# The first modulation set fetched as scale blocks and then shift blocks, channel products in two halves, and the last two expert blocks by columns

## The chip, the cores and the metric

The kernel runs on one NeuronCore of a Trainium2 chip. The metric is the device time of one execution in microseconds (us). Three runs of the kernel before took 1420.25 to 1420.28 us, median 1420.26 us.

## The reference, cut to what matters

Two transformer blocks act on 256 latent and 256 context tokens of 1024 channels, all in float32. The first block has two layers. Layer 0 is an FNet mixer (a DFT over tokens and over channels, then a projection), layer 1 is attention; each is followed by a SwiGLU of 2816. The second block is one mixer (RG-LRU and gated linear attention) and a mixture of 32 experts of which each token uses two, then a last RMS norm.

```python
sh1, sc1, g1, sh2, sc2, g2 = jnp.split(cond_lat @ w_ada[i] + b_ada[i], 6, axis=-1)
h_lat = modulate(rms_norm(x, norm_gain[i, 0]), sh1, sc1)      # y * (1 + sc1) + sh1
o_lat, o_ctx = fnet_mixer(h_lat, h_ctx, fnet_w_out[j], fnet_b_out[j], need_ctx)
x = x + g1 * o_lat
...
hid = jax.nn.silu(xb @ w_gate[e]) * (xb @ w_up[e])            # per expert, on its tokens
y = zeros.at[buf_t].add((hid @ w_down[e]) * buf_w)            # scattered back, weighted
x = x + gt2 * y
return rms_norm_2(x, g_final)
```

Every layer's six modulation vectors (shift, scale and gate, twice) come from a product of a condition vector with a 1024 x 6144 matrix, so the matrix has to be read in full for two columns of data.

## The kernel before

All weights come through one DMA queue (SP) in an order fixed by the list `STREAM`, in blocks of 128 x 2048 floats (1 MB). Each block has a slot; SP waits until the slot's last user has released it and then issues, in order. The other engines (PE, ACT, DVE, POOL) run fixed programs in order too and wait on semaphores, so the order of the code is the order of the work.

**The front.** The first 24 blocks go to eight slots. Their order is: eight blocks `("ada", 0, 0, k)` (k is a depth of 128 rows; the 2048 columns are shift and scale together), `fnet` 0, gate blocks `("ada", 0, 1, 0)` and 1, `fnet` 1, gate blocks 2 and 3, `fnet` 2, `fnet` 3, and eight blocks `("ada", 0, 2, k)`. After `fnet` 2 the tokens `xT` (2 MB) are read by the same queue. PE computes the DFT over tokens (`spectrum(c, streams)`, L977) for eight channel chunks c and two streams (latent, context), from token squares that ACT has made. Between the spectra it takes the `ada` blocks as they land (`ada_rows(n, ks)`, L886: four products of 32 rows a block, eight instructions in the profile, since one float32 matmul is two). When a set is complete, ACT copies the four rows out (`arow_of`, L1826), PE turns them into columns (`ada_cols`, L914 and L916), DVE adds the bias (`mods`, L2400) and, for set 0, makes the gains (L2468). ACT and DVE then scale the spectra by gain into `Z` (L1881, L2532), DVE adds the shift to one column of each chunk (`shift_spectrum`, L2541), and PE does the DFT over channels: `channels(i)` (L987, products of 64 output rows, a cosine and a sine half) and `nyquist` (L992). ACT and DVE split the result into high and low parts (`yh` L1889, `yl` L2555).

POOL folds each `fnet` weight block in four quarters (L2327) as soon as it has landed; ACT and DVE split each quarter in a high part `whi` (L1820) and a low part `wlo` (L2388). PE then runs eight `fnet_chunk(c)` (L1010, L1016), 27 products each; chunks 2b and 2b+1 use `fnet` block b. `MODS` says which `ada_rows` follow which chunk, and `ada_cols(1)` (the gate) comes after chunk 1. ACT and DVE finish each chunk (`join`, `add_fnet`), and the feed-forward follows.

**The experts.** Pairs p = 0 to 15 of experts work side by side, each on 64 slots, as two column groups of the PE array (`side_by_side`, L1627). For a pair: gate and up products, their product turned (L1672), the down product in two halves of 512 columns (`down`, banks 6 and 7), high and low parts of it (ACT `outs` L2282, DVE `outs` L3189), and a scatter back to tokens (`scatter(p, half)`, L1701: eight products into the accumulators of four chunks). Twelve blocks of 1 MB go through per pair. The last four blocks of the stream, `LAST`, are each sent as two DMAs of half a block.

**The tail.** PE: `down(15)` half 0, half 1, `scatter(15, 0)`, `scatter(15, 1)`, then eight sums of squares (`pe_sums`, L865). DVE adds each chunk to x (`added_last`, L3118), ACT squares it (L1831), and after the sums makes the root (L1840, L1842); DVE normalises (`normed(6)`, L2492, eight operations), and SP stores three pieces.

Of the kernel before, what the change touches and what calls it, by code (L numbers as in the profile page):

```python
# [15 lines left out]
P = 128  # L16
# [79 lines left out]
PE_ROWS = {0: range(8), 1: range(4), 2: range(8), 6: range(2), 7: range(1), 8: range(1)}  # L96
# [3 lines left out]
MOD_STREAMS = {n: 2 if n in (0, 1, 2, "g2", 3) else 1 for n in ORDER}  # L100
TWO_DEPTHS = (1, "g2")
# [34 lines left out]
LAST = MOE[-4:]  # L136
LOWER_FIRST = {0: False, 2: False, 6: True, 8: True, 12: True, 14: True, 16: True, 18: True}
# [57 lines left out]
def program(nc, wblk, cols_d, cons_d, small_d, wa2_d, xin_d, xnat_d, dft_d, wny_d, rope_d, out_d):  # L195
    ctx = ExitStack()
    with ctx:
# [262 lines left out]
        s_zero = signal("cleared", [("cact",), ("wny",), ("eps",), ("pick",), ("lx",), ("sT",)])  # L460

        events = []
        for n, (layer, s) in enumerate(SETS):
            if n == 3:
                events.append([("sum", "g2"), ("rows", "g2")])
            mine = [[(n, k)] for k in PE_ROWS.get(n, ())] + [[("sum", n)]] * (layer > 0)
            mine[-1].append(("rows", n))
            events += mine
# [7 lines left out]
        def modulated(layer, s, chunk6):  # L476
            return s_mod.at(3 * layer + chunk6 // 2 if layer else (0, 0, 1, 2, 2, "g2")[chunk6], s)
# [3 lines left out]
        s_sqa = signal("squares_act", [(r, c) for r in range(1, 5) for c in ACT_SQUARES[r]] + [(6, c) for c in range(KC)])  # L481
# [5 lines left out]
        triples = [(r, c, s) for r in (1, 2, 3, 4, 6) for c in range(KC) for s in range(len(NORM_STREAMS[r]))]  # L487
        s_ny = signal("normed", triples)
# [9 lines left out]
        s_d1 = signal("dft_tokens", [(c,) for c in range(KC)])  # L498
        ACT_SCALED, DVE_SCALED = (0, 2, 4, 6, 7), (1, 3, 5)
# [92 lines left out]
        r_sc = signal("r_scattered", [(p, half) for p in range(NP) for half in range(2)])  # L592
# [9 lines left out]
        r_oh = signal("r_out_high", [(p, half) for p in range(NP) for half in range(2)])  # L602
        r_ol = signal("r_out_low", [(p, half) for p in range(NP) for half in range(2)])
# [33 lines left out]
        def turned_rows(n):  # L637
            return bank[{0: 7, 6: 5}.get(n, 6)]
# [139 lines left out]
        def sync(e):  # L778
            def used(tag):
                if tag[0] == "fnet":  # L780
                    e.wait_ge(*s_fold.at(tag[1], 3))
                elif tag[0] == "ada":
                    signal = s_adv if tag[1] == 1 else s_adw if tag[1] == 2 and tag[2:] in WEIGHED else s_adam
                    if tag[1:3] == (0, 3):
                        e.wait_ge(*s_adv.at("g2", tag[3]))
                    else:
                        e.wait_ge(*signal.at(3 * tag[1] + tag[2], tag[3]))
# [81 lines left out]
        def pe(e):  # L869
# [4 lines left out]
            def ada_rows(n, ks):  # L874
                layer, s = SETS[n]
                for k in ks:
                    tag = ("ada", layer, s, k)
                    w = block_of(tag)
                    e.wait_ge(*landed(tag))
                    if k == 0 and n:  # L880
                        e.wait_ge(*s_arow.at(n - 1))
                        if n == 1:
                            e.wait_ge(*s_za.at(7))
                    for g in range(4):
                        depth = 2 * k + g // 2 if n == 1 else k
                        t = e.matmul(bank[7][32 * g:32 * g + 32, :], cact[:, 1 if layer == 2 else 0, depth, :], w[:, g * 512:(g + 1) * 512],  # L886
                                     start=k == 0, stop=k == (3 if n == 1 else 7), skip_group_check=layer == 2)
# [140 lines left out]
            spectrum(3, (1,))  # L1028
            spectrum(4, (0,))
            ada_rows(0, (4,))  # L1030
            spectrum(4, (1,))
            ada_rows(0, (5,))
            spectrum(5, (0,))
            ada_rows(0, (6,))
# [12 lines left out]
            channels(3)  # L1047
            nyquist(1)
            ada_rows(1, range(1, 2))
            MODS = {0: (1, range(2, 4)), 3: (2, range(1)), 4: (2, range(1, 3)), 5: (2, range(3, 5)), 6: (2, range(5, 6))}  # L1050
            for c in range(KC):
# [3 lines left out]
                if c == 1:  # L1055
# [558 lines left out]
        def pe_routed(e):  # L1614
# [67 lines left out]

            def down(p):
                lhs = lambda k, i: hidT[:, p % 2, k, 64 * i:64 * i + 64]
                e.wait_ge(*r_hidT.at(p))
                for half in range(2):
# [5 lines left out]
                    if p == NP - 1 and half:  # L1692
                        scatter(p, 0)


# [9 lines left out]
            for p in range(NP + 2):  # L1705
# [7 lines left out]
                if p > NP:  # L1713
                    scatter(NP - 1, 1)
# [13 lines left out]
            pe_sums(e, 6)  # L1728
# [1687 lines left out]
```

## Time and profile before

| | |
|---|---|
| median of three runs | 1420.26 us |
| the profiled execution's own time | 1419.94 us |
| its span, first to last instruction | 1418.0 us |
| PE busy | 1379.8 us (97%) |
| DVE, ACT, POOL busy | 789.1, 524.2, 75.8 us |
| granted TensorE clock, mean | 0.998 |
| HBM | 388.01 MB read, 274 GB/s over the span |

The span runs from the first to the last instruction; the remaining 1.94 us of the profiled execution lie around it. Busy time of PE is modelled from pipelined starts, so it says where PE had nothing to do rather than how well it was used. In the front and in the expert stage the DMA engines are busy throughout; between them they are not.

### The profile page before, as it was taken

Reading aid. Unit: us, or ns where it says so; the run is one execution under the profiler, and the core shown is the slowest. Engines: PE = TensorE matmul, PEld = TensorE weight load, DVE = VectorE, ACT = ScalarE, POOL = GpSimd, SP = SyncE. Lnnn points to the kernel's source line nnn. Section 1 sums busy time; section 2 is a strip of 40 time slices with the busy share of each in tenths; the row PEclk is TensorE's granted clock in tenths of the full one; section 3 lists DMA queues with packets and bytes.
Section 4 is the critical chain, followed back from the end, with each engine's and each line's share of the span. In section 5 each row is a group of like instructions: output and inputs, shape, how many; then the busy total and the mean of one; then the engine's idle time right before and its main releaser. Section 6 shows DMA issues by size and latency. Waiting matters only on the chain.

```text
span 1418.0 us, 20093 instructions
## 1 busy us (share of the span) xinstructions
PE 1379.8 (97%) x8038; PEld 994.2 (70%) x8038; DVE 789.1 (56%) x1402; ACT 524.2 (37%) x1099; POOL 75.8 (5%) x74
## 2 busy tenths in 40 slices
PE   7999999999999999999999999999999999999987
PEld 4767887888887998888888998996444444443433
DVE  1978796665666886667788778684212112112113
ACT  2643222223444555445556666852111111111102
POOL 0600000000002141000000000010000000000000
PEclk9999999999999999999999999999999999999999
DMA  9958666764443332013687454478999999999995
GB/s 391 425 220 314 237 249 256 267 241 174 167 175 119 149 129 81 31 60 117 264 340 318 150 208 178 179 305 324 425 432 428 430 430 428 429 432 429 430 427 224
DMA packets 48130, 390.42 MB, mean 275 GB/s; under 512 B 5256, under 2 KB 6552, under 8 KB 9376
## 3 DMA queue, kind: packets, MB, share of 16 engines
q1 hardware_dynamic: 47408, 387.70, 68.1%
q8 instruction: 66, 1.08, 0.3%
q10 hardware_dynamic: 624, 1.37, 0.2%
q14 instruction: 32, 0.26, 0.1%
HBM read 388.01 MB, written 1.05 MB: 274 GB/s over the span
## 4 chain that ended last, share of the span: by engine, by line
PE 85%; DMA 8%; DVE 3%; ACT 2%; issue 1%; SPq 0%; DVEq 0%; ACTq 0%
PE twin L966 41%; PE twin L1627 19%; DMA ring<-in_wblk 6%; PE twin L1064 5%; PE twin L1065 3%; PE twin L1701 2%; DMA front_ring<-in_wblk 2%; PE twin L1610 2%; PE twin L1010 2%; PE twin L1480 2%; PE twin L1305 1%; PE twin L1241 1%; PE twin L1265 1%; DVE wlo L2388 1%; PE twin L886 1%
## 5 line engine op out<-in xcount | busy, mean ns | idle before, releaser
L2388 DVE TENSOR_TENSOR wlo<-ring,whi 128x512 fp32r<-128x512 f32 (+1 forms) x392 | 254.4, 697 | 64.7 <-ACT whi L1820 61.7
L1820 ACT ACTIVATE whi<-ring 128x512 fp32r<-128x512 f32 (+1 forms) x392 | 216.8, 611 | 106.7 <-PE twin L966 86.4
L966 PE MATMUL twin<-H,whi 128*128 128x512 f32 x700 | 216.3, 390 | 0.1
L966 PE MATMUL twin<-hsp,whi 128*128 128x512 f32 (+1 forms) x704 | 172.5, 337 | 1.8 <-DVE hsp L2587 0.9
L1627 PE MATMUL twin<-ring,xg 128*64 128x512 f32 x696 | 158.3, 597 | 8.4 <-DMA ring<-in_wblk 8.0
L966 PEld LDWEIGHTS twin<-H,whi 128*128 128x128 f32 x700 | 130.8, 188 | 30.1 <-issue 2.5
L966 PE MATMUL twin<-H,wlo 128*128 128x512 f32 x350 | 136.2, 389 | 0.0
L966 PEld LDWEIGHTS twin<-hsp,whi 128*128 128x128 f32 x704 | 120.7, 190 | 17.0 <-DVE wlo L2388 1.7
L1064 PE MATMUL twin<-H,whi 128*128 128x512 f32 x350 | 124.2, 400 | 0.5 <-DVE H L2485 0.2
L966 PE MATMUL twin<-hsp,wlo 128*128 128x512 f32 (+1 forms) x352 | 118.3, 336 | 0.0
L1627 PEld LDWEIGHTS twin<-ring,xg 128*64 128x64 f32 x696 | 48.0, 137 | 97.0 <-issue 88.2
L1627 PE MATMUL twin<-ring,xT 128*64 128x512 f32 x456 | 102.0, 595 | 2.5 <-DMA ring<-in_wblk 2.0
L3174 DVE TENSOR_TENSOR rst<-rst,twin 128x512 f32<-128x512 f32 x16 | 11.0, 688 | 166.4 <-issue 161.2
L1065 PE MATMUL twin<-H,wlo 128*128 128x256 f32 x350 | 98.3, 281 | 0.0
L966 PE MATMUL twin<-whi,Hh 128*128 128x256 f32 x304 | 88.3, 291 | 0.0
L966 PE MATMUL twin<-wlo,Hh 128*128 128x256 f32 x304 | 85.9, 283 | 0.0
L966 PE MATMUL twin<-whi,Hl 128*128 128x256 f32 x304 | 85.9, 283 | 0.0
L3189 DVE SCALAR_TENSOR_TENSOR outs<-twin,tiny,outs 128x512 fp32r<-128x512 f32 x32 | 24.0, 751 | 104.6 <-ACT outs L2282 52.8
L1064 PEld LDWEIGHTS twin<-H,whi 128*128 128x128 f32 x350 | 65.8, 188 | 17.6 <-DVE H L2485 0.6
L2587 DVE TENSOR_TENSOR hsp<-hid,hsp 128x512 fp32r<-128x512 f32 (+1 forms) x88 | 49.1, 563 | 50.5 <-ACT hsp L1928 50.5
L1928 ACT ACTIVATE hsp<-hid 128x512 fp32r<-128x512 f32 (+1 forms) x88 | 45.5, 524 | 84.6 <-PE twin L966 84.6
L1627 PEld LDWEIGHTS twin<-ring,xT 128*64 128x64 f32 x456 | 32.1, 137 | 62.4 <-issue 62.3
(428 smaller groups left out, 2375.6 us busy)
## 6 DMA issues: line engine op xcount, KB each, us to landing
ring<-in_wblk SPq DMA_DIRECT2D x213, 1024.0 KB, 6.1
ring<-in_wblk SPq DMA_DIRECT2D x56, 2048.0 KB, 30.6
front_ring<-in_wblk SPq DMA_DIRECT2D x12, 1024.0 KB, 19.1
small<-in_wblk SPq DMA_DIRECT2D x10, 1024.0 KB, 26.4
tmp<-in_wblk SPq DMA_DIRECT2D x9, 1024.0 KB, 23.8
ring<-in_wblk SPq DMA_DIRECT2D x12, 512.0 KB, 18.8
xnat<-in_xnat SPq DMA_DIRECT2D x4, 512.0 KB, 6.7
xT<-in_xin SPq DMA_DIRECT2D x1, 2048.0 KB, 23.4
```

What stands on the lines that cost most here:

```text
L966: t = e.matmul(out, a, b, start=start and n == 0, stop=stop and n == 2)
L1010: e.matmul(out[:, r], ws[x][:, k, m * P:(m + 1) * P], y[:, i, r], start=k == 0 and n == 0, stop=k == KC - 1 and n == 2, skip_group_check=True)
L1064: e.matmul(b[:, :].rearrange("p (x n) -> p x n", x=2), w[0], FHB[1][:, :, k, :], start=start, stop=stop, skip_group_check=True)
L1065: return e.matmul(b[:, 0:L], w[1], FH[1][0][:, k, :], start=False, stop=stop, skip_group_check=True)
L1480: t = e.matmul(wout_bank(b, m)[:, m * L:(m + 1) * L], ws[i][:, k, m * P:(m + 1) * P], XM[j][:, k, :], start=k == 0 and (m == 0 or b == 3) ...
L1610: t = e.matmul(gather_bank(q, j)[:, i * 256:(i + 1) * 256], h2[n % 2][:, n // 2, c * P:(c + 1) * P], Gs[:, n // 2, :], start=n == 0, stop= ...
L1627: t = e.matmul(like(out[64 * i:64 * i + 64, :], rows), lhs(kcs + kk, i), rows, start=start and kk == 0, stop=stop and kk == 3)
L1701: t = e.matmul(acc(c), osp[:, part_, c * P:(c + 1) * P], Sw[:, p % 2, :], start=p == 0 and part_ == 0 and c % 2 == 0, stop=p == NP - 1 and ...
L1820: e.activation(hi, w, ACT.Copy).then_inc(*s_hi.up(m, h))
L1928: e.activation(hsp[:, k % nsp, 0, 0:n], hid[:, k, 0:n], ACT.Copy).then_inc(*s_hph.up(layer, half, k))
L2388: e.tensor_tensor(lo, w, hi.bitcast(F32), ALU.subtract).then_inc(*s_lov.up(m, h))
L2587: e.tensor_tensor(hsp[:, k % nsp, 1, 0:n], hid[:, k, 0:n], hsp[:, k % nsp, 0, 0:n].bitcast(F32), ALU.subtract).then_inc(*s_hpl.up(layer, h ...
```

## The change

Set 0 is split in two sets that are fetched one behind the other in the same eight places of the stream: four blocks with the scale (each two depths of 1024 columns), then four with the shift. Their rows, columns and `mods` become two steps; the shift has bank 4. Gains and scaled spectra need the scale alone. `channels(i)` is split in the sine half (which no shift touches) and the cosine half. The order of spectra begins with chunk 4. Five products of cleared data go ahead of the first spectrum, and POOL clears their operand first. `MODS` moves some set 1 and set 2 rows one chunk later, and `ada_cols(1)` to behind chunk 2.

The last two blocks hold columns 512 to 767 and 768 to 1023 of both experts' down weights over the whole depth, where they held half the depth of 512 columns. `scatter(15, 0)` is put between the two column products, and the second half's scatter is split in two, with two of the sums of squares between. ACT takes squares 0 to 3 ahead of the last high part, and makes x times final gain for chunks 0 to 3 after it; DVE normalises these four in one operation.

```diff
-ADA0 = {0: (0, 2), 1: (2, 1), 2: (3, 2), "g2": (5, 1)}
-ORDER = [0, 1, 2, "g2", 3, 4, 5, 6, 7, 8]
+ADA0 = {0: (1, 1), "shift": (0, 1), 1: (2, 1), 2: (3, 2), "g2": (5, 1)}
+ORDER = [0, "shift", 1, 2, "g2", 3, 4, 5, 6, 7, 8]
...
+                    if k == 0 and n == "shift":
+                        e.wait_ge(*s_za.at(4))
...
-            def channels(i):
-                e.wait_ge(*s_dc.at(2 * i + 1))
-                for table, r, n0, n1 in ((cd, EVEN, 127, 256), (sd, ODD, 0, 127)):
-                    for j in range(2):
-                        t = e.matmul(streams(spectrum_bank[i][64 * j:64 * j + 64, r]), table, Z[:, 2 * i + j, :, n0:n1], start=True, stop=True)
-                t.then_inc(*s_d2.up(i))
+            def channels(i, r):
+                if r == ODD:
+                    for c in (2 * i, 2 * i + 1):
+                        e.wait_ge(*(s_za if c in ACT_SCALED else s_zv).at(c))
+                else:
+                    e.wait_ge(*s_dc.at(2 * i + 1))
+                table, n0, n1 = (sd, 0, 127) if r == ODD else (cd, 127, 256)
...
-            for c in range(4):
+            e.wait_ge(*s_zero.at("warm"))
+            for _ in range(5):
+                e.matmul(bank[6][:, :], rst[:, 0, 0:P], rst[:, 0, :], start=True, stop=True)
+            for c in (4, 0, 1, 2, 3):
                 spectrum(c, (0,))
+            spectrum(4, (1,))
+            e.wait_ge(*s_cond.at("c2"))
+            ada_rows(0, (0,))
             spectrum(0, (1,))
-            e.wait_ge(*s_cond.at("c2"))
-            ada_rows(0, range(2))
             spectrum(1, (1,))
+            ada_rows(0, (1,))
+            spectrum(2, (1,))
             ada_rows(0, (2,))
-            spectrum(2, (1,))
+            spectrum(3, (1,))
+            spectrum(5, (0,))
             ada_rows(0, (3,))
...
             spectrum(5, (1,))
-            ada_rows(0, (7,))
-            spectrum(6, (0,))
             e.wait_ge(s_cons, 16)
             ada_cols(0)
-            spectrum(6, (1,))
-            spectrum(7)
-            channels(0)
-            channels(1)
+            spectrum(6)
+            spectrum(7, (0,))
+            ada_rows("shift", (0,))
+            spectrum(7, (1,))
+            ada_rows("shift", (1, 2))
+            channels(0, ODD)
+            ada_rows("shift", (3,))
+            channels(1, ODD)
+            ada_cols("shift")
+            channels(2, ODD)
+            channels(3, ODD)
+            channels(0, EVEN)
+            channels(1, EVEN)
             nyquist(0)
-            channels(2)
+            channels(2, EVEN)
             ada_rows(1, range(1))
-            channels(3)
+            channels(3, EVEN)
             nyquist(1)
             ada_rows(1, range(1, 2))
-            MODS = {0: (1, range(2, 4)), 3: (2, range(1)), 4: (2, range(1, 3)), 5: (2, range(3, 5)), 6: (2, range(5, 6))}
+            MODS = {0: (1, range(2, 3)), 1: (1, range(3, 4)), 3: (2, range(1)), 4: (2, range(1, 2)), 5: (2, range(2, 4)), 6: (2, range(4, 6))}
             for c in range(KC):
                 fnet_chunk(c)
                 if c in MODS:
                     ada_rows(*MODS[c])
-                if c == 1:
+                if c == 2:
                     ada_cols(1)
...
+            def last_columns(a):
+                tag = LAST[2 + a]
+                rows = block_of(tag)[:, :].rearrange("p (k i n) -> p k i n", k=4, i=2)
+                out = bank[5 if a else 7][:, 0:L]
+                e.wait_ge(s_upper[2 + a], 16)
+                for k in range(4):
+                    if k == 2:
+                        e.wait_ge(*landed(tag))
+                    for i in range(2):
+                        t = e.matmul(out[64 * i:64 * i + 64, :], hidT[:, (NP - 1) % 2, k, 64 * i:64 * i + 64], rows[:, k, i, :], start=k == 0, stop=k == 3)
+                t.then_inc(*s_rel.up(*tag))
...
-                    if p == NP - 1 and half:
-                        scatter(p, 0)
+                if p == NP - 1:
+                    e.wait_ge(*r_ol.at(p - 1, 1))
+                    last_columns(0)
+                    scatter(p, 0)
+                    last_columns(1)
...
                 if p > NP:
-                    scatter(NP - 1, 1)
+                    scatter_last(0)
+                    pe_sums(e, 6, range(2))
+                    scatter_last(1)
...
-            pe_sums(e, 6)
+            pe_sums(e, 6, range(2, KC))
...
-                if c == 0:
+                if c == 1:
                     arow_of(1)
...
+            def last_gained():
+                for c in range(4):
+                    t = e.activation(xg[:, c, :], xT[:, c, 0:L], ACT.Copy, scale=NORM_A[6, 0][:, c:c + 1])
...
         def pool(e):
+            e.memset(rst[:, 0, :], 0.0).then_inc(*s_zero.up("warm"))
...
+            def last_normed():
+                e.wait_ge(*s_root.at(6))
+                e.wait_ge(*s_sqa.at("gained"))
+                e.tensor_tensor(hM[:, 0:4, :], xg[:, 0:4, :], rst[:, 0, 0:L].unsqueeze(1).broadcast_to([P, 4, L]), ALU.mult).then_inc(*s_ny.up(6, 3, 0))
+                for c in range(4, KC):
+                    e.scalar_tensor_tensor(hM[:, c, :], xT[:, c, 0:L], NORM_A[6, 0][:, c:c + 1], rst[:, 0, 0:L], ALU.mult, ALU.mult).then_inc(*s_ny.up(6, c, 0))
```

## Rows read from the trace of the kernel before

**Rows 1.** The page: the chain that ended last, by engine.

```profile
PE 85%; DMA 8%; DVE 3%; ACT 2%; issue 1%; SPq 0%; DVEq 0%; ACTq 0%
```

**Rows 2.** Timeline of PE, 0 to 75 us: start, length, instructions [idle before, releaser].

```profile
9.54 7.21 PE L977 MATMUL twin<-fs,xnat 128*128 128x256 f32 x20 [9.54 <-DVE fs L2509]
16.68 1.92 PE L886 MATMUL twin<-ring,small 128*32 128x512 f32 x16
18.53 1.13 PE L977 MATMUL twin<-fs,xnat 128*128 128x256 f32 x4
19.59 1.06 PE L886 MATMUL twin<-ring,small 128*32 128x512 f32 x8
...
31.63 1.06 PE L886 MATMUL twin<-front_ring,small 128*32 128x512 f32 x8 [0.82 <-DMA front_ring<-in_wblk]
...
33.60 0.60 PE L916 MATMUL twin<-cons,small 128*128 128x128 f32 x4
34.03 2.76 PE L977 MATMUL twin<-fs,xnat 128*128 128x256 f32 x12
36.72 2.17 PE L987 MATMUL twin<-Z,dft 128*64 128x258 f32 x16
...
43.85 0.39 PE L1010 MATMUL twin<-yh,whi 128*128 128x258 f32 x1
...
47.75 1.92 PE L886 MATMUL twin<-front_ring,small 128*32 128x512 f32 x16
49.60 0.39 PE L1010 MATMUL twin<-yh,whi 128*128 128x258 f32 x1
...
52.94 0.96 PE L914 MATMUL twin<-cons,small 128*128 128x8 f32 x8
...
60.39 1.06 PE L886 MATMUL twin<-ring,small 128*32 128x512 f32 x8
```

**Rows 3.** Timeline of POOL, 0 to 70 us.

```profile
0.73 0.52 POOL L2311 MEMSET small<- 128x512 f32 x1 [0.29 <-POOLq L3296]
...
33.93 4.97 POOL L2327 TENSOR_TENSOR fold<-ring 128x512 f32<-128x512 f32 x4 [31.53 <-DMA ring<-in_wblk]
41.24 6.36 POOL L2327 TENSOR_TENSOR fold<-ring 128x512 f32<-128x512 f32 x4 [2.33 <-DMA ring<-in_wblk]
...
56.11 8.52 POOL L2327 TENSOR_TENSOR fold<-front_ring 128x512 f32<-128x512 f32 x4 [1.33 <-DMA front_ring<-in_wblk]
```

**Rows 4.** Timeline of ACT, 0 to 80 us.

```profile
5.57 1.06 ACT L1863 ACTIVATE Z<-xnat 128x1024 f32<-128x1024 f32 x1 [0.62 <-DMA xnat<-in_xnat]
...
32.77 0.60 ACT L1826 ACTIVATE small<-twin 128x512 f32<-128x512 f32 x1 [18.38 <-PE twin L886]
```

**Rows 5.** Timeline of DVE, 0 to 80 us.

```profile
14.42 1.23 DVE L2511 TENSOR_TENSOR wnl<-tmp,wnh 128x1024 fp32r<-128x1024 f32 x1 [1.76 <-ACT wnh L1875]
34.24 0.26 DVE L2400 TENSOR_TENSOR mod<-twin,cols 128x16 f32<-128x16 f32 x2 [18.59 <-PE twin L916]
...
41.42 1.64 DVE L2388 TENSOR_TENSOR wlo<-fold,whi 128x512 fp32r<-128x512 f32 x1
```

**Rows 6.** Timeline of PE in the expert stage, 1270 to 1388 us.

```profile
1313.65 3.65 PE L1627 MATMUL twin<-ring,xg 128*64 128x512 f32 x16 [2.71 <-DMA ring<-in_wblk]
```

**Rows 7.** Timeline of PE, 1385 us to the end.

```profile
1394.28 2.38 PE L1701 MATMUL twin<-Sw,outs 128*128 128x256 f32 x16
1396.59 7.09 PE L1627 MATMUL twin<-ring,xT 128*64 128x512 f32 x32
1403.60 2.38 PE L1701 MATMUL twin<-Sw,outs 128*128 128x256 f32 x16
1406.09 3.72 PE L865 MATMUL twin<-xT,cons 128*128 128x256 f32 x16
```

**Rows 8.** Stretches of 1 us at the end: length, engines' busy, granted clock, DMA share, GB/s.

```profile
1400.00:1401.00 1.00, 1.00 (x8) 0.36 (x6) 0.00 (x0) 0.66 (x1) 0.00 (x0) 1.00 0.12 49
```

**Rows 9.** Timeline of DVE, 1385 us to the end.

```profile
1410.87 3.25 DVE L2492 SCALAR_TENSOR_TENSOR hTm<-xT,cols,rst 128x256 f32<-128x256 f32 x8 [2.55 <-ACT rst L1842]
```

More of the change, by code:

```diff
@@ L136 @@
 LAST = MOE[-4:]
+OUT_PARTS = [(p, half) for p in range(NP) for half in range(2)][:-1] + [(NP - 1, 1, a) for a in range(2)]
 LOWER_FIRST = {0: False, 2: False, 6: True, 8: True, 12: True, 14: True, 16: True, 18: True}
@@ L465, in program @@
                 events.append([("sum", "g2"), ("rows", "g2")])
+            if n == 1:
+                events += [[("shift", k)] for k in range(3)] + [[("shift", 3), ("rows", "shift")]]
             mine = [[(n, k)] for k in PE_ROWS.get(n, ())] + [[("sum", n)]] * (layer > 0)
@@ L476, in modulated @@
         def modulated(layer, s, chunk6):
-            return s_mod.at(3 * layer + chunk6 // 2 if layer else (0, 0, 1, 2, 2, "g2")[chunk6], s)
-        s_sqa = signal("squares_act", [(r, c) for r in range(1, 5) for c in ACT_SQUARES[r]] + [(6, c) for c in range(KC)])
+            return s_mod.at(3 * layer + chunk6 // 2 if layer else ("shift", 0, 1, 2, 2, "g2")[chunk6], s)
+        s_sqa = signal("squares_act", [(r, c) for r in range(1, 5) for c in ACT_SQUARES[r]] + [(6, c) for c in range(4)] + [("gained",)] + [(6, c) for c in range(4, KC)])
         s_sqv = signal("squares_dve", [(r, c) for r in range(1, 5) for c in range(KC - 1) if c not in ACT_SQUARES[r]] + [(5, KC - 1)])
@@ L497, in program @@
         s_a0 = signal("fnet_scales", [(0,)])
-        s_d1 = signal("dft_tokens", [(c,) for c in range(KC)])
-        ACT_SCALED, DVE_SCALED = (0, 2, 4, 6, 7), (1, 3, 5)
+        s_d1 = signal("dft_tokens", [(c,) for c in (4, 0, 1, 2, 3, 5, 6, 7)])
+        ACT_SCALED, DVE_SCALED = (4, 0, 2, 6, 7), (1, 3, 5)
         s_za = signal("spectrum_scaled_act", [(c,) for c in ACT_SCALED])
@@ L591, in program @@
         r_spp = signal("r_spread", [(p,) for p in range(NP)])
-        r_sc = signal("r_scattered", [(p, half) for p in range(NP) for half in range(2)])
+        r_sc = signal("r_scattered", OUT_PARTS)
         r_sel = signal("r_selected", [(0, 0), (0, 1)] + [(q,) for q in range(1, 8)])
@@ L601, in program @@
         r_gs = signal("r_slot_weights", [(p,) for p in range(NP)])
-        r_oh = signal("r_out_high", [(p, half) for p in range(NP) for half in range(2)])
-        r_ol = signal("r_out_low", [(p, half) for p in range(NP) for half in range(2)])
+        r_oh = signal("r_out_high", OUT_PARTS)
+        r_ol = signal("r_out_low", OUT_PARTS)
         d_dg = signal("d_diagonals", [("dg",)])
@@ L637, in turned_rows, with rows_bank @@
         def turned_rows(n):
-            return bank[{0: 7, 6: 5}.get(n, 6)]
+            return bank[{0: 7, "shift": 4, 6: 5}.get(n, 6)]
+        def rows_bank(n):
+            return bank[4 if n == "shift" else 7]
         def unit_turned(u):
@@ L785, in used @@
                         e.wait_ge(*s_adv.at("g2", tag[3]))
+                    elif tag[1:3] == (0, 0) and tag[3] >= 4:
+                        e.wait_ge(*s_adam.at("shift", tag[3] - 4))
                     else:
@@ L1685, in down @@
                 e.wait_ge(*r_hidT.at(p))
-                for half in range(2):
+                for half in range(1 if p == NP - 1 else 2):
                     if p % 2 == 0 and p < 14:
@@ L1691, in down, with scatter_last @@
                     side_by_side(bank[6 + half], p, "ed", half, 0, lhs, True, True)
-                    if p == NP - 1 and half:
-                        scatter(p, 0)
+                if p == NP - 1:
[3 more added lines that the diff above has]
+                    last_columns(1)
+            def scatter_last(a):
+                for part_ in range(2):
+                    e.wait_ge(*(r_ol if part_ else r_oh).at(NP - 1, 1, a))
+                    for c in range(4 + 2 * a, 6 + 2 * a):
+                        t = e.matmul(acc(c), osp[:, part_, c * P:(c + 1) * P], Sw[:, (NP - 1) % 2, :], start=False, stop=part_ == 1,
+                                     skip_group_check=True)
+                t.then_inc(*r_sc.up(NP - 1, 1, a))
             def scatter(p, half):
@@ L1825, in arow_of @@
                     e.wait_ge(*s_adat.at(BEFORE[i]))
[L1826 removed]
+                e.activation(arow[:, :], rows_bank(i)[:, :], ACT.Copy).then_inc(*s_arow.up(i))
             def square(r, c, ready):
@@ L1886, in act @@
                 scale_spectrum(c)
+            arow_of("shift")
             for i in range(4):
@@ L2278, in act_routed @@
                     for half in range(2):
+                        if (p, half) == (NP, 1):
+                            e.wait_ge(*r_sc.at(p - 2, half))
+                            for a in range(2):
+                                if a:
+                                    before_last()
+                                e.wait_ge(*s_rel.at(*LAST[2 + a]))
+                                e.activation(osp[:, 0, 512 + a * L:512 + (a + 1) * L], bank[5 if a else 7][:, 0:L], ACT.Copy,
+                                             scale=gslot[:, (NP - 1) % 2:(NP - 1) % 2 + 1]).then_inc(*r_oh.up(NP - 1, 1, a))
+                            break
                         e.wait_ge(*s_rel.at("ed", 2 * p - 1, half))
@@ L2543, in dve @@
             e.wait_ge(*s_a0.at(0))
-            scale_spectrum(1)
-            shift_spectrum(0)
-            shift_spectrum(1)
-            scale_spectrum(3)
-            shift_spectrum(2)
-            shift_spectrum(3)
-            scale_spectrum(5)
-            for c in range(4, KC):
+            for c in DVE_SCALED:
+                scale_spectrum(c)
+            mods("shift")
+            e.wait_ge(*s_mod.at("shift", 1))
+            for c in range(KC):
                 shift_spectrum(c)
@@ L3183, in dve_routed @@
                     e.wait_ge(*r_gs.at(p - 1))
-                    for half in range(2):
+                    for half in range(1 if p == NP else 2):
                         r = slice(half * 512, (half + 1) * 512)
@@ L3194, in dve_routed, with low_last @@
                     slot_weights(p + 1)
-            for half in range(2):
-                e.wait_ge(*r_sc.at(NP - 1, half))
-                for c in range(4 * half, 4 * half + 4):
-                    added_last(c)
+            def low_last(a):
+                r = slice(512 + a * L, 512 + (a + 1) * L)
+                e.wait_ge(*r_oh.at(NP - 1, 1, a))
+                e.scalar_tensor_tensor(osp[:, 1, r], bank[5 if a else 7][:, 0:L], gslot[:, (NP - 1) % 2:(NP - 1) % 2 + 1], osp[:, 0, r].bitcast(F32),
+                                       ALU.mult, ALU.subtract).then_inc(*r_ol.up(NP - 1, 1, a))
+            low_last(0)
+            e.wait_ge(*r_sc.at(NP - 1, 0))
+            for c in range(4):
+                added_last(c)
+            low_last(1)
+            for a in range(2):
+                e.wait_ge(*r_sc.at(NP - 1, 1, a))
+                added_last(4 + 2 * a)
+                added_last(5 + 2 * a)
         def dve_dense(e):
```

81 lines of the change are left out of this document (46 added, 35 removed).

## The prediction

> **What bounds the kernel now.** I read the page's chain first: 85% of the path that ends last is PE and 8% DMA [rows 1]. So an edit counts only if it shortens PE's list of work where PE never waits, or brings forward what PE does wait for. The change touches the first 60 us and the last 18. What lies between is tied together: SP issues a block when its slot is released, so an earlier PE gives earlier transfers. The expert stage too, where PE waits for blocks (2.71 us at 1313.65 [rows 6]), moves along as a whole, since its transfers start on released slots. I take a gain in the front to arrive at the end in full.
>
> In the front, PE's timeline [rows 2] shows a list that is nearly dense from 9.54 us, with three losses. The first 20 spectrum products take 7.14 us to the next start, 0.357 each, against 0.224 (2.69 / 12) at 34.03: 2.66 us lost, which looks like 1.2 GHz for most of that stretch and 2.4 GHz after. At 31.63 PE waits 0.82 us for the eighth block. Chunk 0 takes 3.90 us (43.85 to 47.75), chunk 1 3.34: 0.56 us of waits for low parts.
>
> The transfers have a clock of their own. POOL starts each fold when its block lands: 41.24 and 56.11, with six blocks' worth between (two gate blocks, `fnet` 2, 2 MB of `xT`, `fnet` 3) [rows 3], or 2.48 us a block. The change leaves that order as it is. So the first block of set 2, next in the stream, lands at about 56.11 + 2.48 = 58.6 us whatever PE does. PE takes it at 60.39 now.
>
> In the tail PE is dense again [rows 7]: half 1 of the last down product starts at 1396.59 + 7.01 / 2 = 1400.10, the scatters at 1403.60, the sums at 1406.09, ending about 1409.81. That is 9.71 us, of which the scatters have 2.49 where the same 16 took 2.31 at 1394.28, so 0.18 is waiting. DMA has sunk to a share of 0.12 by 1400 to 1401 [rows 8]: the last blocks are there before PE needs them.
>
> **The front, step by step.** I count PE's list up to the start of chunk 3. Before: columns of the gate at 52.94, 0.85 us (0.96 less the overlap with the next), chunk 2 3.34, so 57.13.
> - The five products on cleared data. They go ahead of 9.54, where PE is idle. If they raise the clock, 2.66 us go. Ten instructions of 512 columns at the slow rate would take 0.357 x 2 x 10 = 7.1 us or a little more, from 1.3 us on (one more memset like the 0.52 us one [rows 3]), so they are over by about 8.5 to 9.5. They cost nothing, up to 0.4 us if they run over. The gap to the first spectrum is 0 to 1 us. PE came out of the 2.71 us wait at full rate (16 in 3.65 us [rows 6]), so the gap alone should not lose the clock. POOL's other clears come 0.52 us later; ACT has 0.62 us of waiting for tokens there [rows 4], so nothing, at most 0.5.
> - Scale first. Its four blocks are in 4 x 2.48 us before the eighth, about 21.7. Gains and scaled spectra are made under other spectra. The 0.82 us go, since PE has other work when the eighth block lands.
> - Added: set 0's columns are eight instructions for four transposes (0.85 for 0.43), +0.42, and the shift's columns +0.85. ACT's copy of the shift rows (0.60 [rows 4]) is covered by one sine half, 0.54 (a quarter of 2.17): +0.15. `mods` and two shift steps (0.26 for two `mods` [rows 5]) lie under two more sine halves.
> - More changes of kind: four spectrum instructions standing alone take 1.06 for 0.90, a lone block's rows 1.0 for 0.925. Some five more such seams: +0.5 (bounds 0 and 1).
> - Waits of chunk 0: the shift's chain ends earlier against it, -0.56, at least 0.
>
> Sum: 57.13 - 2.66 - 0.82 - 0.56 + 0.42 + 0.85 + 0.15 + 0.5 = 55.0. Chunk 3 ends at 58.35. There PE wants the first block of set 2, which lands at 58.6. So the front gives 60.39 - 58.6 = **1.8 us**, not the 2.1 that PE's list saves; the transfer becomes the bound. The later blocks (61.1, 63.5, 66.0, 68.5, 71.0) are wanted from 62.9, 67.3 and 72.5 on, so they don't wait. The gate's `mods` now comes behind chunk 2, at about the same time as before on the clock, so DVE's additions lose their lead; the chunks that need them (low parts for 4 and 6) start 1.8 earlier but still after.
>
> **The tail.** PE: the two column products are 16 instructions each, 64 rows by 256 columns. No such row stands here; from below half the pace of the 512-column ones, 7.01 / 64 x 16 = 1.75, from above the channel products, 64 rows by 258 columns, 2.17 [rows 2]. I take 1.95, nearer the middle because those channel products also waited for DVE. PE then needs 3.9 + 2.31 + 3.72 = 9.93 for 9.71: **+0.22** (from -0.2 to +0.66). Moving `scatter(15, 0)` and two sums ahead only reorders a list with 0.18 us of air in it. ACT stays within: its 256-column pieces at 0.4 (under the 0.60 of 512) begin squares at 3.5 after 1400.10, and reach the last square at 8.7, when the last sum starts at 9.46. The four gain products there cost nothing, but 0.7 is all the room.
>
> DVE: eight normalisations take 3.25, 0.41 each [rows 9]. Four of them become one operation of 1024 columns on SBUF data. The like of it took 1.23 [rows 5]; bounds 0.6 (twice that rate) and 1.63 (no gain). With 1.23 the end comes **0.40** sooner. The stores follow. Tail: -0.18 (from -1.2 to +0.66).
>
> **Sum.** 1419.94 (the profiled execution's own time) - 1.80 - 0.18 = 1417.96. The median of the runs is 0.32 above that execution, so 1418.3.
>
> **Where a page would have it otherwise.** The first rows show slow instructions at the start and the expert rows none behind a wait. The Trainium skill (TensorE: Matmul & The Clock Gate, Part 1: The HAM clock gate) says that the throttled clock is the default, released by activity and resumed after idling. By that the products help, if the pause behind them is short; the trace agrees for the long-running array. Low parts show DVE held while POOL folds: 1.64 at 41.42, as POOL began at 41.24 [rows 3, 5]. The Trainium skill (SBUF - State Buffer, SBUF: two separate sides) calls the port pair of the two an exclusive lock for a whole instruction; the third rival is what that would do here.
>
> **The rivals.**
> - *PE's list bounds and is shorter than I sum.* The seams cost nothing (54.5 rather than 55.0) and the first block of set 2 lands a little ahead of the pace. Front 2.6, tail 0.5 with the column products at their lower bound: 3.1, so 1417.2. For it: the landing is inferred, not seen. Against: 2.48 holds over six blocks.
> - *The clock does not rise, or falls again before 9.54.* This is the one on the other side. The list is 2.66 longer, chunk 3 starts at 57.7 and ends at 61.0 where 60.39 stood: +0.6, tail -0.18, so 1420.7. It decides as soon as less than about 0.6 us of the 2.66 is won. For it: two sets of columns are added, and nothing in the trace shows how cleared data acts.
> - *Low parts are late.* Block 0's folding runs 33.93 to 38.90 and block 1's from 41.24 [rows 3], under DVE's high-low work, which now begins some 3 us earlier. If each of the four quarters is held 0.5 to 1 us (1.24 a fold quarter), chunk 0 or 2 waits about 1.4, of which 0.25 is free: 1419.4.
> - *Column products don't run side by side.* Each 256-column instruction at 0.224: 3.6 each, +3.3 on the tail, so 1421.6. Against: the channel products, in the same two groups, do.
>
> **How the numbers follow.** Forecast 0.60 (own range 1417.7 to 1418.9), the shorter list 0.17, low parts 0.10, the clock 0.09, columns 0.04. The likeliest gives 1418.3. The range 1417.0 to 1420.0 leaves out the clock, the columns and the far end of the shorter list. A measurement of this kernel tells 0.2%, 2.84 us, from no change: faster means below 1417.42. That is the shorter list and a corner of the forecast, 0.22; slower, above 1423.1, needs two mishaps, 0.02; same 0.76.
>
> **What would show it.** First 20 spectrum products at 0.224 each from 9.54. PE idle on DMA for some 0.3 us ahead of the first set 2 rows, at 58.6, and none at 31.6. Chunk 0 near 42. Columns 1.95 each; the sums' end 9.9 after the last pair's half 0; one DVE operation of 1.2 us. I am wrong if PE takes that block later than 59.2 or before 58.0, or if the tail from half 0's end to the last normalisation changes by over 0.7.

## The result, and the profile after

The changed kernel takes 1420.84 us (median of 17 runs, 1418.80 to 1424.89), the kernel before in runs on the same chip 1419.22 (17 runs). The ratio is 1.0015, with a 95% interval of 1.0009 to 1.0022: 2.1 us slower (1.3 to 3.1), where 2.0 faster was forecast. The two medians alone differ by 1.6. The profiled execution took 1423.76 us, with a span of 1421.3.

The first thing on the page is the chain of waits by engine, which answers to [rows 1]:

```profile
PE 87%; DMA 6%; DVE 4%; ACT 2%; issue 1%; SPq 0%; DVEq 0%; ACTq 0%
```

DMA has given up two points, and PE and DVE have taken them. So the question is what PE does more of, and where DVE came onto the path. PE's timeline from the start (start, length, instructions, and in brackets the idle time before them with its releaser) answers to [rows 2]:

```profile
1.31 5.97 PE L1036 MATMUL twin<-rst 128*128 128x512 f32 x10 [1.31 <-POOL rst L2382]
9.27 5.45 PE L987 MATMUL twin<-fs,xnat 128*128 128x256 f32 x24 [1.99 <-DVE fs L2581]
14.65 1.07 PE L896 MATMUL twin<-ring,small 128*32 128x512 f32 x8
...
36.59 0.66 PE L1001 MATMUL twin<-Z,dft 128*64 128x258 f32 x4 [0.17 <-DVE Z L2613]
37.82 0.66 PE L1001 MATMUL twin<-Z,dft 128*64 128x258 f32 x4 [0.57 <-DVE Z L2613]
...
42.65 0.39 PE L1025 MATMUL twin<-yh,whi 128*128 128x258 f32 x1
...
54.98 0.96 PE L924 MATMUL twin<-cons,small 128*128 128x8 f32 x8
55.79 0.37 PE L1025 MATMUL twin<-yh,whi 128*128 128x258 f32 x1
...
59.19 1.06 PE L896 MATMUL twin<-ring,small 128*32 128x512 f32 x8
62.64 0.58 PE L1025 MATMUL twin<-yh,whi 128*128 128x258 f32 x1 [2.39 <-DVE wlo L2460]
63.02 0.42 PE L1025 MATMUL twin<-yl,whi 128*128 128x258 f32 x1
```

Down to 59.19 the front does nearly what was forecast: the first 24 spectrum products are over in 5.38 us, chunk 0 begins at 42.65 (43.85 before), and the first rows of set 2 at 59.19 (60.39 before). Then comes a wait that the kernel before does not have: 2.39 us for a low part of `fnet` block 2. And the first products behind it start 0.215 us apart instead of 0.12. The stretches of 1 us around it (length; busy time and instructions of PE, PEld, DVE, ACT, POOL; granted clock; DMA share; GB/s) show why:

```profile
62.00:63.00 1.00, 0.36 (x1) 0.36 (x2) 1.00 (x2) 0.63 (x1) 0.00 (x0) 0.61 1.10 467
63.00:64.00 1.00, 1.00 (x6) 1.00 (x6) 1.00 (x3) 0.00 (x0) 0.00 (x0) 0.50 1.01 426
64.00:65.00 1.00, 1.00 (x7) 1.00 (x6) 1.00 (x3) 0.00 (x0) 0.00 (x0) 0.50 0.97 410
65.00:66.00 1.00, 1.00 (x8) 1.00 (x8) 0.96 (x4) 0.00 (x0) 0.00 (x0) 0.68 1.05 442
```

The granted clock is 0.50, which is 1.2 GHz, for some 3.4 us; it falls at 62.2, while PE still waits. Thirteen products of chunk 4 run at that pace, which costs 13 x (0.215 - 0.12) = 1.2 us. Wait and clock together are 3.6 us, against the 1.2 that the front had gained at 59.19.

What DVE does meanwhile stands in its timeline, here of the kernel before:

```profile
54.47 0.23 DVE L2400 TENSOR_TENSOR mod<-twin,cols 128x8 f32<-128x8 f32 x2
54.74 1.67 DVE L2527 SCALAR_TENSOR_TENSOR xT<-tmp,mod,xT 128x256 f32<-128x256 f32 x4
56.33 2.49 DVE L2388 TENSOR_TENSOR wlo<-fold,whi 128x512 fp32r<-128x512 f32 x4
```

and of the kernel after, with POOL's last fold among it:

```profile
55.97 0.24 DVE L2472 TENSOR_TENSOR mod<-twin,cols 128x8 f32<-128x8 f32 x2 [3.79 <-PE twin L924]
56.09 5.62 POOL L2399 TENSOR_TENSOR fold<-front_ring 128x512 f32<-128x512 f32 x4 [1.70 <-DMA front_ring<-in_wblk]
56.24 5.74 DVE L2599 SCALAR_TENSOR_TENSOR xT<-tmp,mod,xT 128x256 f32<-128x256 f32 x4
61.91 2.48 DVE L2460 TENSOR_TENSOR wlo<-fold,whi 128x512 fp32r<-128x512 f32 x4
```

The same four additions take 1.67 us before POOL's fold and 5.74 us under it, 1.43 each, as long as one quarter of the fold (5.62 / 4 = 1.41). In the kernel before, the fold began at 56.11 [rows 3], while DVE was still in the last addition, and DVE went on to the low parts at 56.33 without a break. They kept their 0.62 each, and it was POOL that waited: the first quarter of its fold took 3.88 us, and the whole fold 8.52. After the change POOL is first by 0.15 us, and DVE waits. The first quarter alone, before and after:

```profile
56.11 3.88 POOL L2327 TENSOR_TENSOR fold<-front_ring 128x512 f32<-128x512 f32 x1 [1.33 <-DMA front_ring<-in_wblk]
```

```profile
56.09 1.31 POOL L2399 TENSOR_TENSOR fold<-front_ring 128x512 f32<-128x512 f32 x1 [1.70 <-DMA front_ring<-in_wblk]
```

The low parts for chunk 4 stand behind the additions in DVE's program, so PE waits too.

The tail answers to [rows 7] and [rows 9]; first PE, then DVE:

```profile
1403.13 1.90 PE L1714 MATMUL twin<-ring,xT 128*64 128x256 f32 x16
1404.96 1.21 PE L1745 MATMUL twin<-Sw,outs 128*128 128x256 f32 x8
1406.09 1.95 PE L1714 MATMUL twin<-ring,xT 128*64 128x256 f32 x16
1407.97 0.74 PE L1736 MATMUL twin<-Sw,outs 128*128 128x256 f32 x4
...
1409.89 2.75 PE L873 MATMUL twin<-xT,cons 128*128 128x256 f32 x12
...
1413.63 1.22 DVE L3192 TENSOR_TENSOR hTm<-xg,rst 128x1024 f32<-128x1024 f32 x1 [2.67 <-ACT rst L1895]
1414.78 1.66 DVE L3194 SCALAR_TENSOR_TENSOR hTm<-xT,cols,rst 128x256 f32<-128x256 f32 x4
```

From 1403.13, where the columns begin, to DVE's end at 1416.44 are 13.31 us. Before, from half 1 at 1400.10 to 1414.12, they were 14.02. That is 0.71 less. But from DVE's end to the end of the span it is now 4.86 us, where it was 3.88.

### The profile page after: what moved, and what is told of

It is laid out like the page before. It is cut to its first block, busy times and chain, and to the rows that moved or that the text cites. A ratio compares the mean times of both kernels' runs of the same rounds, so it can differ in the third digit from the quotient of the medians.

```text
span 1421.3 us, 20182 instructions
## 1 busy us (share of the span) xinstructions
PE 1388.2 (98%) x8076; PEld 999.3 (70%) x8076; DVE 792.0 (56%) x1402; ACT 527.5 (37%) x1105; POOL 72.9 (5%) x75
## 3 DMA queue, kind: packets, MB, share of 16 engines
q8 instruction: 66, 1.08, 0.3%
## 4 chain that ended last, share of the span: by engine, by line
PE 87%; DMA 6%; DVE 4%; ACT 2%; issue 1%; SPq 0%; DVEq 0%; ACTq 0%
PE twin L976 41%; PE twin L1649 19%; DMA ring<-in_wblk 6%; PE twin L1086 5%; PE twin L1087 3%; PE twin L1745 2%; PE twin L1632 2%; PE twin L1025 2%; PE twin L1502 2%; PE twin L896 1%; PE twin L1327 1%; PE twin L1263 1%; PE twin L987 1%; PE twin L1287 1%; DVE wlo L2460 1%
## 5 line engine op out<-in xcount | busy, mean ns | idle before, releaser
L2460 DVE TENSOR_TENSOR wlo<-ring,whi 128x512 fp32r<-128x512 f32 (+1 forms) x392 | 254.4, 697 | 65.2 <-ACT whi L1873 62.2
L1649 PE MATMUL twin<-ring,xT 128*64 128x512 f32 x440 | 98.4, 595 | 2.0 <-DMA ring<-in_wblk 2.0
L976 PEld LDWEIGHTS twin<-H,wlo 128*128 128x128 f32 x350 | 65.7, 188 | 13.8
```

The source lines that it names most:

```text
L976: t = e.matmul(out, a, b, start=start and n == 0, stop=stop and n == 2)
L1649: t = e.matmul(like(out[64 * i:64 * i + 64, :], rows), lhs(kcs + kk, i), rows, start=start and kk == 0, stop=stop and kk == 3)
L2460: e.tensor_tensor(lo, w, hi.bitcast(F32), ALU.subtract).then_inc(*s_lov.up(m, h))
```

## The experiments

Two marks place each run's differences: the start of ACT's last operation on chunk 7's product (the end of the front), and the length from the start of half 1 or the columns to the end of the span (the tail). All ratios are to the kernel before on the same chip. The second run of the changed kernel, gate back, fold waits and tail only were measured on one chip, the four others on a second; the kernel before took 1419.29 us (median of 33 runs) on either. The first row of the changed kernel is the result above, against its own 1419.22. The measured differences are the ratio's, times 1419.3.

| kernel | chunk 7 mark | against before | tail | ratio [95%] | difference, us |
|---|---|---|---|---|---|
| before | 79.83 | | 17.90 | 1 | |
| after | 82.42 | +2.59 | 18.17 | 1.0015 [1.0009, 1.0022] | +2.1 |
| after, again | 82.51 | +2.68 | 18.17 | 1.0010 [1.0000, 1.0021] | +1.4 |
| gate back | 78.27 | -1.56 | 18.36 | 0.9988 [0.9979, 0.9997] | -1.7 |
| fold waits | 78.52 | -1.31 | 18.05 | 0.9989 [0.9980, 0.9998] | -1.6 |
| low parts first | 78.58 | -1.25 | 17.46 | 0.9993 [0.9984, 1.0002] | -1.0 |
| gate back, old tail | 78.29 | -1.54 | 17.8 | 0.9991 [0.9982, 1.0000] | -1.3 |
| gate back, no warm | 79.73 | -0.10 | 17.98 | 1.0004 [0.9995, 1.0013] | +0.6 |
| no warm | 81.31 | +1.48 | 18.44 | 1.0011 [1.0002, 1.0020] | +1.6 |
| tail only | 79.87 | +0.04 | 17.96 | 0.9992 [0.9983, 1.0001] | -1.1 |

**The changed kernel once more.** No edit. Could the wait be an accident of one execution?

> The changed kernel once more, on the chip of the next three, to see which of its stretches come back. Theory (lock): DVE's four additions of chunks 0 and 1 again run against POOL's fold of the last fnet block and take 5 to 6 us (1.67 before), and PE waits 2 to 2.5 us for the low parts of fnet block 2 ahead of chunk 4. Rival (chance): that wait is not there again, and what was slow were the low-clock spells at 929 and 1318 us. By the theory 1.001 to 1.002 of the kernel before, by chance anything from 0.998.

It was not. PE's row in the profile of this run:

```profile
62.53 0.39 PE L1025 MATMUL twin<-yh,whi 128*128 128x258 f32 x1 [2.37 <-DVE wlo L2460]
```

The additions took 5.72 us and the clock fell again behind the wait. This profile's span was 1419.1. The stretch from the mark to the tail took 2.3 us less than in the first profile, which had two more spells of low clock in it (929 to 936 and 1318 to 1322 us). Such spells come and go from run to run; the front's loss is in both profiles.

**Gate back.** The gate's columns again behind chunk 1, with its last block of rows and ACT's copy of the rows one chunk earlier too; the rest of the change kept.

```diff
-            MODS = {0: (1, range(2, 3)), 1: (1, range(3, 4)), 3: ...  # (cut)
+            MODS = {0: (1, range(2, 4)), 3: ...  # (cut)
...
-                if c == 2:
+                if c == 1:
                     ada_cols(1)
...
-                if c == 1:
+                if c == 0:
                     arow_of(1)
```

> The changed kernel with both late gate blocks behind chunk 0 and the gate's columns behind chunk 1, as before. The additions then start some 3.5 us earlier, about 52.5, and are done before POOL starts its last fold at 56.1. Lock theory and the rival that the columns are simply too late both expect the additions in 1.7 us, no wait ahead of chunk 4, chunk 7 over some 3.5 to 4 us earlier than in the changed kernel, and 0.9975 to 0.999 of the kernel before. If the spells of low clock in the middle were the cause, it stays at 1.001.

Measured 1418.37 us. DVE again gets the additions done ahead of the fold, and PE never waits between 55 and 66 us (PE and DVE in order of time):

```profile
51.40 0.96 PE L924 MATMUL twin<-cons,small 128*128 128x8 f32 x8
...
53.59 2.19 DVE L2599 SCALAR_TENSOR_TENSOR xT<-tmp,mod,xT 128x256 f32<-128x256 f32 x4 [0.43 <-DVE mod L2472]
55.70 2.48 DVE L2460 TENSOR_TENSOR wlo<-fold,whi 128x512 fp32r<-128x512 f32 x4
...
58.83 1.06 PE L896 MATMUL twin<-ring,small 128*32 128x512 f32 x8
```

The low parts start at 55.70, ahead of POOL's fold at 56.04, and it is again the fold's first quarter that waits (3.33 us). So the gate's place turns 2.1 us of loss into 1.7 of gain. It does not yet say whether the columns' lateness is enough, or whether the overlap with POOL is needed.

**Fold waits.** The columns stay late. POOL's last fold starts only when the second chunk has been added, so that the overlap alone is gone.

```diff
                 if b >= 2:
                     e.wait_ge(*s_lov.at(b - 2, 3))
+                if b == 3:
+                    e.wait_ge(*s_fnx.at(1, 1))
```

> The changed kernel, with POOL's fold of the last fnet block held until DVE's four additions are done; the gate's columns stay behind chunk 2. Lock theory: the additions start at 56.2 as in the changed kernel but take 1.7 us, DVE's split ends about 60.3, the first low part is there at 58.5, PE waits nothing ahead of chunk 4; POOL folds from 58 to 63.6, early enough for chunk 6. Chunk 7 ends 3.5 us earlier than in the changed kernel; 0.9975 to 0.999 of the kernel before. Rival (columns too late by themselves): the wait ahead of chunk 4 stays at 2 us or more and the time at 1.001.

DVE and POOL of this kernel:

```profile
55.86 0.24 DVE L2474 TENSOR_TENSOR mod<-twin,cols 128x8 f32<-128x8 f32 x2 [3.79 <-PE twin L924]
56.13 1.68 DVE L2601 SCALAR_TENSOR_TENSOR xT<-tmp,mod,xT 128x256 f32<-128x256 f32 x4
57.72 2.49 DVE L2462 TENSOR_TENSOR wlo<-fold,whi 128x512 fp32r<-128x512 f32 x4
...
57.98 8.06 POOL L2401 TENSOR_TENSOR fold<-front_ring 128x512 f32<-128x512 f32 x4 [3.71 <-DVE xT L2601]
```

This is the run that decides, by one added wait. The additions start as late as in the changed kernel (56.13 for 56.24), but take 1.68 us instead of 5.74. The low parts start at 57.72, PE goes from set 2's rows at 59.08 straight into chunk 4 at 60.07, and its clock stays up. The kernel is faster than before by 1.6 us. On the same chip the changed kernel's median was 1421.35, this one's is 1418.18. Against gate back (1418.37) nothing is lost by being late; what the changed kernel loses comes with the overlap. The fold itself, from 57.98 on, took 8.06 us, and PE did not wait for anything made from it.

**Low parts first.** The other way round: the overlap stays, but DVE makes `fnet` block 2's low parts ahead of the additions.

```diff
             join(1)
+            split(12)
             mods(1)
...
             add_fnet(1)
-            split(12)
```

> The changed kernel with DVE's low parts of fnet block 2 ahead of the gate's mods and the additions of chunks 0 and 1. Lock theory: the low parts are there by 55.5, the additions still start at 56.2 and still take 5.7 us against POOL's fold, but PE doesn't wait for them ahead of chunk 4, nor for the next low parts ahead of chunk 6 (about 69 against a start at 69.7, so a wait of up to 0.5 us can show). Chunk 7 ends at 78.5 to 79; 0.9985 to 0.9995 of the kernel before. Rival (additions late hold up the rest of DVE's list): a wait of over 1 us moves to chunk 6 and the time stays at 1.001.

DVE of this kernel:

```profile
52.89 3.63 DVE L2460 TENSOR_TENSOR wlo<-fold,whi 128x512 fp32r<-128x512 f32 x4 [0.76 <-ACT whi L1873]
...
56.70 5.62 DVE L2599 SCALAR_TENSOR_TENSOR xT<-tmp,mod,xT 128x256 f32<-128x256 f32 x4
```

The additions are held just as long, 5.62 us, and PE does not wait (59.13, then chunk 4 at 60.13). Median 1417.40 us, the lowest of all, though the interval still touches no change. So a slow DVE operation is no cost by itself. It became one because four low parts that PE wants at 60.2 stood behind it.

**No warm.** Without the five products on cleared data and their wait, everything else as changed. What are they worth?

> The changed kernel without the five products on cleared data ahead of the first spectrum (POOL's clearing stays). The first 24 spectrum products then take some 8 us, not 5.4, and PE's list reaches chunk 4 about 2.6 us later, near 62.8. Lock theory: DVE's low parts for that chunk come at 62.6 or a little later anyway, so the wait of 2.4 us shrinks to under 1, the low clock behind it goes too, chunk 7 is over at 81 to 82.5 (82.42 in the changed kernel), and the whole takes the same as the changed kernel or up to 1 us less. Rival (PE's list sets the front): 2.6 us slower than the changed kernel, 1.003 of the kernel before.

PE and DVE of this kernel in order of time:

```profile
9.59 7.50 PE L987 MATMUL twin<-fs,xnat 128*128 128x256 f32 x24 [9.59 <-DVE fs L2578]
...
57.76 4.43 DVE L2596 SCALAR_TENSOR_TENSOR xT<-tmp,mod,xT 128x256 f32<-128x256 f32 x4
...
60.70 1.06 PE L896 MATMUL twin<-ring,small 128*32 128x512 f32 x8
62.11 2.48 DVE L2457 TENSOR_TENSOR wlo<-fold,whi 128x512 fp32r<-128x512 f32 x4
...
62.85 0.39 PE L1025 MATMUL twin<-yh,whi 128*128 128x258 f32 x1 [1.08 <-DVE wlo L2457]
```

The 24 products take 7.43 us instead of 5.38, and PE comes to set 2's rows 1.5 us later. But the low parts come when POOL's fold lets DVE go, at 62.11 against 61.91. The 1.5 us that the warm products gave had only made the wait longer, 2.39 instead of 1.08, and with 1.08 the clock did not fall. So the front ends 1.1 us earlier without them. In the medians (1420.78, and 1420.84 and 1421.35 with them) the two kernels are not told apart.

**Gate back, no warm.** Both edits. Here the same five products have nothing behind them that eats their gain.

> The kernel with the gate's columns back behind chunk 1, without the five products. There the low parts are early, so PE's list counts: it reaches the first rows of set 2 about 2.1 us later than with them (60.9 for 58.8, where the block's landing held it), and chunk 7 ends near 80.4 against 78.27. Time 2 us above that kernel: ratio 1.000 to 1.001 of the kernel before. Rival (the products buy nothing anywhere): 0.9988 as with them.

The mark is at 79.73 for 78.27: 1.46 us, and in the medians 1419.63 for 1418.37 (on two chips; by the ratios it is 2.3, and the two intervals just overlap). Worth some 1.3 us in one version and nothing, or less, in the other.

**Tail only.** The new tail on the kernel before.

> The tail of the change alone on the front of the kernel before. From the start of the last down product's second half to DVE's last operation 13.3 us, as in the changed kernel, against 14.0 before (PE's list 9.5 for 9.7, normalising 2.8 for 3.25). Theory: the whole is 0.7 us faster, ratio 0.9995, as the stores take 3.9 us as before. Rival: the stores take 4.9 us, as in the changed kernel's profile, since the third is issued late, and the ratio is 1.000 or above.

From the columns to DVE's end it is 13.31 us, to the hundredth what the changed kernel has. The median is 1418.85 us, -1.1 us with an interval of -2.4 to +0.1; the profile's tail as a whole is no shorter than before (17.96 for 17.90).

**Gate back, old tail.** The tail tested from the other side: the gate-back kernel with the tail of before.

> The kernel with the gate's columns back behind chunk 1, and the tail of the kernel before. From the start of the last down product's second half to DVE's last operation 14.0 us, against 13.3 with the new tail. First theory: the new tail is worth its 0.7 us, so this is 0.7 us slower than the kernel with the gate back (1418.4). Second theory: the stores end at a time of their own, 18.0 to 18.4 us behind that start with either tail, and the two kernels are equal within 0.3 us.

1418.11 us against 1418.37 with the new tail: no difference that can be told. In the profiles, what DVE saves is used up behind it. The span ends 4.1 to 5.1 us behind DVE's last operation in all eight profiles with the new tail, and 3.8 and 3.9 in the two with the old one. The issues of the three stores on SP's queue took 3.21 us in the gate-back kernel and 2.39 in this one.

A longer issue does not explain it. In the no-warm kernel it took 2.03 us, and the span still ended 5.1 us behind DVE. Nothing else was tried on the stores, so this stays open.

## Why the prediction was wrong

The step that failed is this one: "The gate's `mods` now comes behind chunk 2, at about the same time as before on the clock, so DVE's additions lose their lead; the chunks that need them (low parts for 4 and 6) start 1.8 earlier but still after." It holds three errors.

- *The time.* `mods` started 1.5 us later (55.97 for 54.47). The prediction's own sum said so: chunk 3 at 55.0 less 0.85 puts the columns at 54.15, against 52.94 before. The lead that the additions had over the fold's 56.11 was 1.4 us, and it was not set against this.
- *The price.* The additions were carried at their old duration. Against the fold they cost 5.74 for 1.67. What decides it is who starts first, here by 0.15 us. The row that shows what such an overlap does was quoted: DVE held for 1.64 at 41.42 where POOL began at 41.24 [rows 3, 5].
- *The deadline.* "Still after" was not a sum. Low parts from 56.3 + 1.5 = 57.8 would have been in time for 60.2, as the fold-waits run shows. From 61.9 they were not.

The third rival had the right mechanism and the wrong place. It looked at the low parts of blocks 0 and 1 and at chunks 0 and 2, priced at 1.4 us, and PE did not wait for low parts there. The loss was at block 3's fold and chunk 4, and cost 3.6. What was missing from it is the second half of the price, the clock that falls behind the wait. The Trainium skill (SBUF - State Buffer, SBUF: two separate sides) states an exclusive lock between GpSimd and a DVE operation with two SBUF inputs, which goes for a whole instruction to whichever starts first. The trace agrees: behind the fold each addition is held for about one of its quarters, 1.43 us, and in the kernel before, where DVE was first, the fold's quarter was held, 3.88 us.

Point by point, the other steps:

- *Warm products raise the clock:* right. 24 in 5.38 us is 0.224 each, the predicted figure, and PE's idle 1.99 us between them and the first spectrum did not lose it. Taken away, the products cost 2.05 us there.
- *PE's list:* chunk 3 at 55.0, measured 55.79. The 0.79 too little are almost all two waits for DVE's shift steps, 0.57 and 0.17, which the sum had put under two sine halves. POOL's fold of block 0 runs over them, and this is the third rival's mechanism once more. Eight steps on 2 columns each take 3.42 us there and 0.66 in the no-warm kernel, where they come as that fold ends (both lines stand in the last section). With the gate back, set 2's rows start at 58.83 for the predicted 58.6.
- *The transfer as the next bound:* not seen. PE never waits for DMA at that place in any of these kernels; its own list bounds it, as the first rival had it, but at a higher sum.
- *The front's gain arrives in full:* not contradicted, in either direction. The marks in the table give the measured differences to within about 1.3 us, half the width of an interval, so they can't confirm it closer than that.
- *The front's gain as such:* 1.8 predicted, 1.56 with the gate back, and -2.59 as changed.
- *Columns:* 1.83 and 1.88 us for the 1.95 predicted, side by side. PE's tail list is 9.51 for 9.93 predicted and 9.71 before.
- *One operation of 1024 columns:* 1.22 for 1.23. Normalising takes 2.81 instead of 3.25, so -0.44 for -0.40. To DVE's end the tail is shorter by 0.71, more than the 0.18 predicted and just past the bound that was set.
- *"The stores follow":* wrong by up to the whole gain. The span ended 4.1 to 5.1 us behind DVE where it was 3.9 before.

The forecast of -1.8 and -0.18 was thus near the gate-back kernel (-1.7), and one chunk's difference in the gate's place separates the two.

## What to carry to other kernels

When a step is moved on one engine, write down for each engine that waits for it the new start, what it then overlaps, and the deadline of whatever stands behind it in that engine's program: here the additions could be late and the low parts could not. An elementwise operation of DVE with both inputs in SBUF that comes behind a running one of POOL was held to the end of POOL's instruction; where DVE's operations were first, POOL waited for their whole unbroken series. So write down which of the two starts first; here it hung on 0.15 us. And a gain ahead of a fixed arrival is no gain: the same five products were worth some 1.3 us in one version and nothing in another.

## What the runs showed of the hardware

**Which side is held depends on who was first, not on the operation.** In three kernels DVE was already at work in a series without a break when the fold began: before (fold at 56.11), gate back (56.04, low parts since 55.70) and fold waits (57.98, low parts since 57.72). The low parts kept their 0.62 us each, and the fold's first quarter took 3.88, 3.33 and 3.41 us, for 1.24 in block 0 of the kernel before. In the first of them that is the 2.7 us up to the last low part's end at 58.8, and then the quarter's own time. In the changed kernel POOL was first. It took 5.62 for its four quarters and let one addition through at each. Nor are others spared that come behind a running quarter: first two low parts of the changed kernel, 0.68 alone, then its eight shift steps, then the same eight without the fold beside them (no warm):

```profile
46.55 1.77 DVE L2460 TENSOR_TENSOR wlo<-fold,whi 128x512 fp32r<-128x512 f32 x1
...
48.85 1.80 DVE L2460 TENSOR_TENSOR wlo<-fold,whi 128x512 fp32r<-128x512 f32 x1
```

```profile
35.73 3.42 DVE L2613 SCALAR_TENSOR_TENSOR Z<-mod,Z 128x2 f32<-128x2 f32 x8
```

```profile
38.09 0.66 DVE L2610 SCALAR_TENSOR_TENSOR Z<-mod,Z 128x2 f32<-128x2 f32 x8
```

**The clock fell behind some waits and not behind others.** It was granted at 0.50 after an idle of 2.39 us (and of 2.37 in the second profile, there 1.3 us after PE had started again), and not after 1.99 at 9.27 or after 1.08 in the no-warm kernel. The length of the wait does not settle it. Near 1313 us PE waits 2.63 to 2.73 us for a block in all ten profiles. Behind this wait the clock stays up in five of them, and the 16 products take 3.65 us [rows 6]. In the other five (changed, gate back, fold waits, gate back without warm products and with the old tail) it falls within 1.5 us of the wait's end, and they take 5.35, as here in the fold-waits kernel:

```profile
1312.52 5.35 PE L1649 MATMUL twin<-ring,xg 128*64 128x512 f32 x16 [2.73 <-DMA ring<-in_wblk]
```

So that the wait at 60.2 makes the clock fall is seen in two profiles of two, but not shown to be a rule. The clock also falls where PE has no idle time at all. Stretches of 2 us of the changed kernel, columns as above:

```profile
927.00:929.00 2.00, 2.00 (x16) 1.79 (x15) 2.00 (x3) 0.39 (x1) 1.40 (x2) 1.00 0.00 0
929.00:931.00 2.00, 2.00 (x11) 1.73 (x9) 1.17 (x1) 0.38 (x1) 0.62 (x1) 0.55 0.00 0
931.00:933.00 2.00, 2.00 (x10) 1.88 (x10) 0.55 (x1) 1.34 (x5) 0.88 (x1) 0.50 0.88 262
```

Small products of 64 columns precede this one. The kernel before has such a spell at 967 to 971, low parts first has none before its end. Mean granted clock and time largely go together over the changed kernel's 17 runs: 1424.89 us at 0.993, 1418.80 at 0.998. The two spells more in the first of its two profiles went with 2.3 us more, as much as the change moves the time.

**The start's slow pace does not show in the granted clock.** In the kernel before, PE starts 4 instructions a microsecond at 10 to 11 us and 7 at 15 to 16, of the same kind, and the column says 1.00 for both:

```profile
10.00:11.00 1.00, 1.00 (x4) 0.73 (x4) 0.00 (x0) 0.88 (x3) 0.00 (x0) 1.00 1.02 425
...
15.00:16.00 1.00, 1.00 (x7) 0.87 (x6) 0.65 (x1) 0.00 (x0) 0.00 (x0) 1.00 0.99 418
```

The pace of the instructions showed it, and taking the warm products away brought the slow pace back. The trace's record of the clock only begins at 14.9 us in the kernel before, at 13.8 in the no-warm kernel and at 4.2 in the changed one, and the column says 1.00 for all time ahead of it. Fitting this, 11.9 products at 0.448 us and 8.1 at 0.224 make the 7.14 us of the first 20, which puts the change of pace at 14.9.
